# The first gather of each expert stage, split in four parts around the first expert's gate and up product

## The reference

```python
g_idx = argmax(xf @ w_group + b_group)             # 1 of 4 groups
top_v, top_i = top_k(e_logits[g_idx], 2)           # 2 of its 8 experts
for each expert e of 32, over the rows that chose it:
    hid = silu(xb @ w_gate[e]) * (xb @ w_up[e])    # 1024 -> 512
    y   = hid @ w_down[e]                          # 512 -> 1024
out[row] += weight * y
```

## Time and profile before

| | us |
|---|---|
| median of three runs | 2009.38 (2008.66 to 2010.47) |
| the profiled execution, device time | 2005.66 |
| its span, first to last instruction | 2003.8 |
| PE busy | 1697.5 (85%) |
| ACT busy | 362.4 (18%) |
| DVE busy | 454.7 (23%) |
| mean granted clock of TensorE | 0.934 |

### The profile page before, as it was taken

The page is one execution under the profiler, slowest core; times in us unless marked ns, Lnnn a source line. Parts: engine busy times, 40 slices in busy tenths (PEclk is TensorE's granted clock), DMA queues, the critical chain, the costliest instruction groups (busy, mean ns, idle before and its releaser), DMA issues.

```text
span 2003.8 us, 17973 instructions
## 1 busy us (share of the span) xinstructions
PE 1697.5 (85%) x7399; PEld 836.3 (42%) x7399; DVE 454.7 (23%) x878; ACT 362.4 (18%) x783; POOL 93.3 (5%) x165
## 2 busy tenths in 40 slices
PE   3996679888888875899979989999897399988988
PEld 1742353333333322654443433333342156554564
DVE  1006530000000002002332000000001433664263
ACT  1003210000000001104321000010000235252352
POOL 1012010000000001013100000000000100010000
PEclk8998879999999998898979999999999599998999
DMA  9988249999999996969339999999997722133320
GB/s 351 360 306 325 85 156 423 424 422 422 422 423 423 421 423 265 372 251 335 123 149 415 422 418 423 417 422 420 418 421 319 262 84 76 38 110 105 123 85 21
DMA packets 122661, 595.20 MB, mean 297 GB/s; under 512 B 9908, under 2 KB 15100, under 8 KB 97992
## 3 DMA queue, kind: packets, MB, share of 16 engines
q1 hardware_dynamic: 96680, 491.93, 60.7%
q0 software_dynamic: 17696, 89.40, 12.2%
q10 hardware_dynamic: 8192, 12.59, 1.7%
HBM read 580.17 MB, written 13.72 MB: 296 GB/s over the span
## 4 chain that ended last, share of the span: by engine, by line
PE 54%; DMA 30%; DVE 8%; ACT 3%; issue 3%; POOL 1%; SPq 1%; ACTq 0%; DVEq 0%; POOLq 0%
PE psum L1846 52%; DMA ring<-in_expert_w_up 23%; DMA ring<-in_expert_w_gate 2%; DMA work<-in_ada_w 2%; DMA ring<-in_ada_w 1%; ACT work L1407 1%; DMA work<-expert_rows,picks 1%; DVE small L904 1%; DVE work L1579 1%; PE psum L1037 1%; DVE work L1580 1%; DVE work L561 1%; DVE work L567 1%; DMA expert_rows<-work 0%; ACT ring L1407 0%
## 5 line engine op out<-in xcount | busy, mean ns | idle before, releaser
L1846 PE MATMUL psum<-ring,work 128*64 128x512 f32 (+5 forms) x4480 | 1169.0, 577 | 95.0 <-DMA ring<-in_expert_w_up 75.7
L1846 PEld LDWEIGHTS psum<-ring,work 128*64 128x64 f32 (+2 forms) x4480 | 453.5, 154 | 728.4 <-issue 700.8
L1846 PE MATMUL psum<-work 128*128 128x192 f32 (+6 forms) x816 | 175.6, 358 | 5.8 <-DVE small L1610 2.0
L1846 PE MATMUL psum<-work,ring 128*128 128x256 f32 (+1 forms) x728 | 166.9, 388 | 3.2 <-ACT work L1407 1.7
L1742 DVE TENSOR_TENSOR work<-work,psum 128x256 f32<-128x256 f32 x64 | 26.9, 421 | 626.3 <-ACT work L1499 626.3
L1846 PEld LDWEIGHTS psum<-work 128*128 128x128 f32 (+2 forms) x816 | 130.9, 207 | 85.8 <-issue 64.4
L1407 ACT ACTIVATE work<-psum 128x256 f32<-128x256 f32 (+5 forms) x237 | 111.4, 482 | 296.2 <-PE psum L1846 112.2
L1499 ACT ACTIVATE work<-psum 128x256 f32<-128x256 f32 x64 | 24.6, 385 | 743.5 <-PE psum L1846 743.5
L1846 PEld LDWEIGHTS psum<-work,ring 128*128 128x128 f32 x728 | 139.5, 196 | 35.5 <-issue 12.3
L1758 DVE TENSOR_TENSOR work<-psum,rows 128x512 f32<-128x512 f32 x64 | 44.2, 691 | 285.8 <-PE psum L1846 285.7
L1846 PE MATMUL psum<-work,small 128*1 128x512 f32 (+1 forms) x512 | 69.7, 633 | 16.2 <-DMA work<-in_ada_w 10.7
(11 more groups left out here) (227 smaller groups left out, 773.0 us busy)
## 6 DMA issues: line engine op xcount, KB each, us to landing
ring<-in_expert_w_gate SPq DMA_DIRECT2D x64, 2048.0 KB, 17.1
ring<-in_expert_w_up SPq DMA_DIRECT2D x64, 2048.0 KB, 21.4
ring<-in_expert_w_down SPq DMA_DIRECT2D x64, 2048.0 KB, 21.1
work<-in_ada_w POOLq DMA_DIRECT2D x40, 1024.0 KB, 8.7
ring<-in_w_in SPq DMA_DIRECT2D x12, 2048.0 KB, 9.3
work<-in_w_mod POOLq DMA_DIRECT2D x16, 1024.0 KB, 5.2
ring<-in_diff_w_in SPq DMA_DIRECT2D x6, 2048.0 KB, 32.0
expert_rows<-work ACTq DMA_DIRECT2D x128, 96.0 KB, 5.6
```

The source lines that it names most:

```text
L1846: return T.matmul(out_, lhsT, rhs, start=start, stop=stop, skip_group_check=True)
```

## The change

The first gather of a layer is cut differently. `FIRST_GATHER` gives four parts: all eight chunks with columns 0 to 63, 512 columns that fill bank 3; chunks 0 to 3 with columns 64 to 191 in bank 4; chunks 4 and 5 with these columns in bank 5; chunks 6 and 7 in bank 6. Parts 0 and 1 stand where the whole gather stood. Parts 2 and 3 stand behind the first expert's gate and up product. PE waits for one copy before that product and for all four before the second expert's; the wait for the four copies ahead of the next group's gather is already in the first expert's turn. ACT copies parts 0 and 1 ahead of its loop and parts 2 and 3 behind the first silu. Later gathers are as they were, and the numbers of semaphore counts stay the same.

```diff
+    FIRST_GATHER = ((range(8), 3, 0, SLOTS), (range(4), 4, SLOTS, QUAD * LIST), (range(4, 6), 5, SLOTS, QUAD * LIST),
+                    (range(6, 8), 6, SLOTS, QUAD * LIST))
 ...
+        def take_first(l, part):
+            ts, b, lo, hi = FIRST_GATHER[part]
+            act.wait_ge(sem("gat_mm"), EACH["gat_mm"] * l + part + 1)
+            copy(hS[:, 0, ts[0]:ts[-1] + 1, lo:hi], bank[b][:, 0:len(ts) * (hi - lo)].rearrange("p (t n) -> p t n", t=len(ts))).then_inc(
+                sem("hS"), 1)
 ...
         def experts(l):                                   # ACT
             act.preload_act_table(ACT.Silu)
-            for c in range(QUAD):
-                take_gathered(l, c, 3 + c)
+            take_first(l, 0)
+            take_first(l, 1)
 ...
                 nc.scalar.activation(s_act, bank[e % 2][:, 0:S], ACT.Silu).then_inc(sem("silu"), 1)
+                if e == 0:
+                    take_first(l, 2)
+                    take_first(l, 3)
 ...
             pe.wait_ge(sem("sel"), EACH["sel"] * l + 1)   # PE, router
-            for c in range(QUAD):
-                for i in range(2):
-                    ins = gather(sel[:, 0], 2 * c + i, bank[3 + c][:, i * S:i * S + QUAD * LIST])
-                ins.then_inc(sem("gat_mm"), 1)
+            gather_first(0).then_inc(sem("gat_mm"), 1)
+            gather_first(1).then_inc(sem("gat_mm"), 1)
+
+        def gather_first(part):
+            ts, b, lo, hi = FIRST_GATHER[part]
+            for t in ts:
+                at_ = (t - ts[0]) * (hi - lo)
+                for tile in range(TT):
+                    ins = mm(bank[b][:, at_:at_ + hi - lo], h[:, tile, t * P:(t + 1) * P],
+                             sel[:, 0, tile].rearrange("p e n -> p (e n)")[:, lo:hi], tile == 0, tile == 1)
+            return ins
 ...
-                if i == 0:
-                    pe.wait_ge(sem("hS"), EACH["hS"] * l + QUAD * (q + 1))
+                if i == 0 or e == 1:
+                    pe.wait_ge(sem("hS"), EACH["hS"] * l + (QUAD * (q + 1) if e else 1))
                 loaded(pe, n0)
                 loaded(pe, n0 + 1)
                 gate_up(n0, hS[:, q % 2, :, i * LIST:i * LIST + SLOTS], e % 2).then_inc(sem("gu"), 1)
+                if e == 0:
+                    gather_first(2).then_inc(sem("gat_mm"), 1)
+                    gather_first(3).then_inc(sem("gat_mm"), 1)
```

## The result

| | before | changed |
|---|---|---|
| median of 22 runs each, us | 2007.46 (2005.69 to 2011.09) | 2012.17 (2008.12 to 2015.96) |
| ratio, with 95% interval | | 1.0022 (1.0015 to 1.0029) |
| profiled execution, device time and span, us | 2005.66, 2003.8 | 2015.12, 2013.3 |

The changed kernel is slower by 0.22%, 4.4 us (the medians differ by 4.7). That is just beyond the 0.2% that counts here as no change, and the interval holds 0.2%; it doesn't hold zero. Its profiled execution is a late one of its kind, and it is already 4.5 us behind at the picks of layer 0, in a part that the change does not touch. So the two traces are compared by stretches that start at the picks (the start of the first gather), never by their ends.

What follows compares the result with a forecast made beforehand. Both expert stages were taken as bound by the weight stream, so its start counts: 0.25 us (layer 0) plus 1.6 (layer 1) gave +1.85, on 2009.38 a forecast of 2011.2 us, range 2007.0 to 2014.6.

Steps and rivals of the forecast that it cites:

- Load-paced records: First gather: weight loads pace 64- and 128-column records, 0.213 us each at the low clock, 10.2 us for 48.
- Rival D: Part 0: columns, not loads, set the pace; -4.1 and -0.8 us, total 2004.5 us; chance 0.04.
- The gap of 0.7 us: Ahead of gate_up(0): some 0.7 us lost to drain, copy and semaphore, which the split removes.
- The clock: First gather: part 0 keeps the clock at 0.50; gate_up(0) starts 1.2 us later in layer 0, 1.6 in layer 1.
- rival C: gate_up(0): clock so late that it starts slow, 8.78 us instead of 7.09; total 2013.3 us; chance 0.14.
- Rival A: First gather: clock rises as early as now; -0.7 us in layer 1, total 2008.5 us; chance 0.23.
- Layer 0: Stream start in the first layer: row and ada_w loads mostly hide 1.2 us of later start; cost 0.25 us.
- The cover of the late release: Behind gate_up(0): third expert's loads cover the fourth pair's later issue; cost nothing, or 1.8 us per layer without cover.
- rival B: Fourth expert: slots released too late, stream runs dry; 1.8 us per layer, total 2014.8 us; chance 0.14.

Runs made afterwards that it cites:

- chunk_wait: Kernel before, gather unchanged, but the first expert's gate and up product waits for the four copies one at a time; ratio to before 1.0005 (0.9994 to 1.0016).
- dummy_more: Kernel before plus 12 unused matmuls on constants (24 records of 128 columns) behind the first gate and up product; ratio to before 1.0013 (1.0002 to 1.0023).
- part0_padded: Changed kernel with part 0 computing 128 columns instead of 64, same records and loads, added columns unused; ratio to before 1.0002 (0.9992 to 1.0012).
- after_again: The changed kernel run once more with no edit; ratio to before 1.0019 (1.0008 to 1.0030).
- warm_late_parts: Changed kernel plus constant matmuls in PE's router idle time, parts 2 and 3 moved behind the first down product; ratio to before 0.9997 (0.9982 to 1.0012).
- wide_first: Changed kernel split at column 128 instead of 64, gate_up(0) waiting for the second copy only at its fifth chunk; ratio to before 1.0009 (0.9998 to 1.0021).
- warm_before: Kernel before plus unused matmuls on constants in PE's idle time of the router; ratio to before 0.9971 (0.9961 to 0.9982).

## Why the prediction was right, and where it was short

The sign and the range held, 2012.17 us in 2007.0 to 2014.6; the forecast of +1.85 us was too small against a measured +4.4. That the forecast time, 2011.2 us, came within 1.0 us is partly luck: the median of the kernel before came out at 2007.46, 1.9 us below the 2009.38 that the forecast was added to. By its steps:

- **Load-paced records, right.** 0.213 us a record at the low clock for both 64 and 128 columns: 7.13 us to the first copy, 10.1 to 10.6 for 48 records, 10.2 forecast. At the full clock 48 take 5.62 us. Rival D, columns as the pace, is out.
- **The gap of 0.7 us, right.** chunk_wait took 0.6 out of the start and the stage.
- **The clock, right, and short in size.** It stayed at 0.50 through part 0 in all three traces of the changed kernel and rose 9.4 to 11.8 us after the picks (before 5.3 to 6.1). The moment isn't set by the gather alone: with the old gather it came at 2.9 us in layer 0 of dummy_more. The term was 1.6 us for layer 1's start; the three traces show 1.4, 2.3 and 2.4, mean 2.0, since in two of them gate_up(0) began at the low clock (7.44 and 7.63 us), which I had left at 7.09. That is rival C's condition, at a part of its price of 1.69 us (8.78 less 7.09). Rival A is out: PE was busy for 6.70 us of 6.70 in part 0 and the clock stayed at 0.50, while in part0_padded, busy alike with twice the columns, it rose. The Trainium skill, "TensorE: Matmul & The Clock Gate", Part 1, says that activity releases the throttle and that the clock follows how busy PE has been. If busy is what the profile counts as busy, this trace doesn't agree.
- **Layer 0, right within its bounds.** I priced it at 0.25; no cost shows, over a spread of 5.8 us in the first issue. The reason given, POOL's ada_w loads that hold the engines meanwhile, was argued from the DMA share (0.98); no run takes these loads away.
- **The cover of the late release: the step that failed.** "So I cost this at nothing" is wrong for two of the three traces of the changed kernel. The insertion was sized well (down load 2.04 us later, 1.8 forecast). What failed is the point at which it can begin to cost. I let it decide when the issue of the fourth expert's pair passes the landing of the third's down load. In the changed kernel it comes 4.9 us ahead of that landing (1073.12 against 1077.99) and the stream thins all the same. A landing follows a load's last packet, and most packets end sooner: 90% of the third down load's had ended 16.4 us behind the first issue, 3.2 us ahead of its landing and only 1.6 after the issue of the pair. That the engines so freed are what thins the stream is argued, not shown. The stream takes 493.7, 492.4 and 493.9 us in the three traces, 493.3 on average against 492.2: +1.1. It looks like rival B's mechanism at less than its price, and in layer 1 alone. Its sign, a DMA share under 0.9 some 17 us behind the first issue, did not come clearly: the share read 0.96 over the window (0.84 in its last 2 us), and the rate, 357 GB/s, is what shows it.

Together: 2.04 + 1.1 = +3.2 us in layer 1's stage (511.2 against 508.0 on average), 0 in layer 0. The whole time says 3.8 to 5.0 us in three comparisons, with lower ends of 3.0, 1.6 and 3.2. The rest, 0.6 to 1.8 us, is not located. The parts outside the stages differ by 8 us between the three traces of the changed kernel (1008.2 to 1016.1 us) and by 1 between the two of the kernel before, in code that is the same in both, so neither chance nor a small effect there is excluded.

What brings the thin stretch is open too. All seven traces with it issued the pair 14.75 us or later behind the first issue, and all six that issued it by 13.96 are without it, which speaks for the late release. after_again, with 14.75, is without it as well, so something else decides there. A rival was not tested: every kernel that delays the releases adds PE instructions on the way, and the traces show a 16 KB packet of the instruction queue (q8) 8.6 to 11.6 us behind the first issue in every kernel with a split gather and at 13.8 in dummy_more, against 18.4 to 21.5 in the six others. after_again has this early packet too (9.7 us), so it isn't enough by itself either. It does go with another difference: the second load of layer 1 lands 14.1 to 14.8 us behind the first issue in every kernel with a split gather, after_again and warm_late_parts among them, and at 12.5 to 13.1 in every one without it, where that packet comes later than this landing. A cause isn't shown by this.

## What to carry to other kernels

Count loads and columns of a matmul apart: cutting one with 192 columns into 64 and 128 saves nothing where, as here, records with 64 and with 128 columns both take 0.213 us behind a 128-wide float32 weight load (192 columns: 0.320). Records of 64 columns also kept the clock low here, so a split that looks shorter ended later. Where a weight stream sets the pace, price a change by two moments, the first issue of the stream and the issues of the next two or three loads: work moved from ahead of the first to behind it can take back all that was won (wide_first: 2.7 us won, 2.9 lost). Take the landing of a load as its last packet's, and look at a second trace of the same kernel before a loss of 1 us is given a cause. Idle time of PE ahead of a critical burst can be used to have the full clock ready for it (warm_before: 5.8 us).

## What the runs showed of the hardware that was not expected

- PE busy for 100% of 6.7 us with 64-column float32 records left the clock at 0.50; with 128 columns in the same records it rose 4.7 us after the start in layer 1 and 2.9 in layer 0.
- The stream lost 0.3 us when the third load was issued 7.04 us behind the first, 1.1 at 7.94 and 2.9 at 9.58 (one trace each), and 1.5, 0.2 and 1.7 us in three traces of one program at 7.84. In the thin stretch, 13.6 to 21.6 us behind the first issue, 16 KB packets took 737 to 786 ns on average, elsewhere 613 to 630, and the DMA share still read 0.96 to 1.01.
- Layer 0's stage did not move by more than 0.6 us while its first issue moved by 5.8.
